# Attention scores from three products of rounded high and low parts, with later query pairs turned in score banks

## The chip, the core and the metric

The program runs on one core of one Trainium2 chip. A core has a matrix engine (TensorE, PE in the profile; PEld is its weight load), a vector engine (VectorE, DVE), an activation engine (ScalarE, ACT), GpSimd (POOL), a queue engine that issues most transfers (SyncE, SP), an on-chip memory of 128 partitions, and eight banks of 128x512 float32 in which matmul results land. The metric is the device time of the whole program in microseconds (us), the median of some runs.

## What is computed

A first block of two layers (retention and gated recurrence, then 16 experts), and a second block of two layers on the same 256 tokens: a pooling layer, then an attention layer, each followed by a multilayer perceptron. The change is in the attention layer:

```
q_l, k_l, v_l = qkv_project(h_lat, w_qkv, g_q, g_k)      # 8 query heads, 2 key heads, 128 wide
q_l = apply_axial_rope(q_l, tables)
k_l = apply_axial_rope(k_l, tables)
q_c, k_c, v_c = qkv_project(h_ctx, w_qkv, g_q, g_k)      # 256 context tokens
k_all = jnp.concatenate([k_c, k_l], axis=1)              # 512 keys
...
s = einsum(q, k) * (HEAD_DIM ** -0.5)
p = softmax(s)
o = einsum(p, v)
```

## The kernel before

Each engine has its instructions written out by hand in one order, and semaphores join them. The expert part runs to about 1380 us and waits mostly for weights. Then come the pooling layer, its perceptron, the attention layer from about 1594 us to 1705 us, and the last perceptron, which runs to the end.

**Attention, ahead of its loop.** PE projects the 256 tokens (two tiles `t` of 128) to keys, values and queries (L1502). DVE norms and rotates the rows (`k_rows`, `q_rows`); the last quarter of the queries is rotated by POOL, after DVE's reciprocal that signals `q_inverse_ready`. PE turns rows to columns by transposes against an identity: `turn_keys` (L1529) fills one bank, which DVE copies to `kT2`, and `turn_queries(pair, bank)` (L1546) fills a bank with two heads, which ACT copies to `qT2` (`query_copies`). The context keys' half of `kT2` was made in the same way during the last expert (`ckT`, L1300).

**The loop.** There are 16 units `u`: 8 heads by 2 tiles of queries. For each, PE forms 128x512 scores in one float32 matmul (`scores(u)`, L1566; a float32 matmul shows as two records). DVE takes the row maximum (`score_max`), ACT the exponential with its sum (`exponentials`), DVE the reciprocal of the sum and the scaling (the row `prob<-prob,softmax_stat`), PE turns the 128x512 result (`turn_probs`, L1575), and ACT copies it to `probT` (`turned_probs`). After each second unit PE multiplies with the values (`values(head)`, L1587). Scores are made two units ahead, in banks 0, 1, 6, 7 in turn; turned probabilities use banks 2 and 3, values banks 4 and 5. Query pair 0 is turned ahead of the loop in bank 2, pair 1 in bank 3, pairs 2 and 3 at units 3 and 7 in bank 5.

```
for u in range(NQ * NT):                      # DVE
    freed(dve, ("s", u))
    step(reciprocal(soft[:, u % 4, 3:4], soft[:, u % 4, 2:3]))
    ts(pr[:, u % 2, :], pr[:, u % 2, :], soft[:, u % 4, 3:4], None, ...
    if u + 2 < NQ * NT:
        score_max(u + 2)
    if u >= 3 and u % 2:
        take_values((u - 3) // 2)
```

After the loop the output product uses rounded parts already: `product` (L628 to L630) adds high times high, high times low and low times high in one bank. A rounded copy has the type `fp32r`.

A bank that `take` hands out again waits until its readers have freed it (`readers` counts them). DVE, ACT and POOL instructions are issued through `InTurn` (L515), so that line stands for most of their rows.

Of the kernel before, what the change touches and what calls it, by code (L numbers as in the profile page):

```python
# [23 lines left out]
ALU = mybir.AluOpType  # L24
# [8 lines left out]
P = 128  # L33
# [19 lines left out]

QUERIES_TURNED = {3: 2, 7: 3}

# [82 lines left out]
def build_program(nc, x, cols, w_in, w_out, w_router, w_gate, w_up, w_down, final_g, ctx_x, w_ada,  # L138
# [144 lines left out]
    rope_c = place("rope2_sb", [P, 2, NT, P])  # L283
    gqk = place("gqk_sb", [P, 2, P])
    x_high = place("x_high", [P, KC, S], F32R, where="xT2")
    x_low = place("x_low", [P, KC, S], F32R, where="x_full")
# [14 lines left out]
    at[0] = here["xs2"]  # L301
    qT2 = place("qT2", [P, NQ, S])
    pr = place("prob", [P, 2, 2 * S])
# [4 lines left out]
    at[0] = here["consts_sb"] + 4 * CONSTS["decay"][0]  # L308
    kT2 = place("kT2", [P, NKV, 2 * S])
    cv = place("ctx_v", [P, NT, NKV * P])  # L310
# [166 lines left out]
    def free(ins, name):  # L477

        ins.then_inc(bank_free[where_is[name][0]], 1)
# [110 lines left out]
    def _(pe):  # L590
# [947 lines left out]
        def turn_queries(pair, bank):  # L1538

            pe.wait_ge(S_("q_rot_ready"), 3 + pair // 2)  # L1540
            name = ("qT", pair)
            ps = take(pe, name, bank)
            for head in (2 * pair, 2 * pair + 1):
                for t in range(NT):
                    at_ = (head % 2) * S + t * P
                    ins = turn(ps[:, at_:at_ + P], qr[:, t, head * P:(head + 1) * P], ident)  # L1546
            fill(ins, name)
# [14 lines left out]
        def scores(u):  # L1562
            head, t = divmod(u, NT)
            name = ("s", u)
            ps = take(pe, name, (0, 1, 6, 7)[u % 4])
            ins = mm(ps[:, :], qT2[:, head, t * P:(t + 1) * P], kT2[:, head // 4, :],  # L1566
                     start=True, stop=True)
            fill(ins, name)
# [37 lines left out]
        for u in range(NQ * NT):  # L1606
# [4 lines left out]
            if u in QUERIES_TURNED:  # L1611
                turn_queries(QUERIES_TURNED[u], 5)
            if u + 2 == NQ * NT:
# [34 lines left out]
    def _(act):  # L1648
# [494 lines left out]
        def query_copies(pair):  # L2143

            name = ("qT", pair)
            ps = full(act, name)
            free(f(qT2[:, 2 * pair:2 * pair + 2, :], ps[:, :].rearrange("p (a t) -> p a t", a=2),
                   ACT.Copy), name)

# [74 lines left out]
    def _(dve):  # L2224
# [113 lines left out]
        for l in range(DEPTH):  # L2338
# [278 lines left out]
            if l == 0:  # L2617
                gains(0, 1, "g_mlp_pre")

            def ctx_normalise():  # L2620
                normalise(NT, lambda t: cx[:, t, :], lambda t: cxn[:, t, :], "ctx_rows_ready",
                          first=2)
# [18 lines left out]
            def ctx_step(e):  # L2641
# [24 lines left out]
                elif (l, e) == (1, 15):  # L2666
                    ps = full(dve, "ckT")
                    free(copy(kT2[:, :, S:2 * S], ps[:, :].rearrange("p (g s) -> p g s", g=NKV)),
                         "ckT")

# [292 lines left out]
        def wo_low(n, q):  # L2963
# [3 lines left out]
            tt(low, whole, high.bitcast(F32), ALU.subtract).then_inc(S_("wo_low_ready"), 1)  # L2967

        k_rows(0)
        even_modulated(1)  # L2970
# [6 lines left out]
        q_rows(1, 0)  # L2977
        ps = full(dve, "kT")
        free(copy(kT2[:, :, 0:S], ps[:, :].rearrange("p (g s) -> p g s", g=NKV)), "kT")
        wo_low(0, 3)  # L2980
        q_sums(1, 1)

# [20 lines left out]
        for u in range(NQ * NT):  # L3003
            freed(dve, ("s", u))
            step(reciprocal(soft[:, u % 4, 3:4], soft[:, u % 4, 2:3]))
            ts(pr[:, u % 2, :], pr[:, u % 2, :], soft[:, u % 4, 3:4], None,
               ALU.mult).then_inc(S_("prob_ready"), 1)
            if u + 2 < NQ * NT:
                score_max(u + 2)
            if u >= 3 and u % 2:  # L3010
                take_values((u - 3) // 2)
# [412 lines left out]
```

## Time and profile before

| what | value |
|---|---|
| median of 3 runs | 1902.17 us (1901.84 to 1902.9) |
| profiled execution, its own time | 1903.21 us |
| span of that execution | 1901.4 us |
| PE busy | 1666.8 us, 88% of the span |
| DVE busy | 797.3 us, 42% |
| ACT busy | 524.6 us, 28% |
| POOL busy | 26.8 us, 1% |
| transfers | 626.74 MB, 330 GB/s on average |

The profile is of one execution. Its own time is the span and 1.8 us that lie around it. A share of busy time is a mean over stages of different kinds: the attention layer, on which the change bears, is about 110 us of the span.

### The profile page before, as it was taken

Reading aid. Unit: us, or ns where it says so; the run is one execution under the profiler, and the core shown is the slowest. Engines: PE = TensorE matmul, PEld = TensorE weight load, DVE = VectorE, ACT = ScalarE, POOL = GpSimd, SP = SyncE. Lnnn points to the kernel's source line nnn. Section 1 sums busy time; section 2 is a strip of 40 time slices with the busy share of each in tenths; the row PEclk is TensorE's granted clock in tenths of the full one; section 3 lists DMA queues with packets and bytes.
Section 4 is the critical chain, followed back from the end, with each engine's and each line's share of the span. In section 5 each row is a group of like instructions: output and inputs, shape, how many; then the busy total and the mean of one; then the engine's idle time right before and its main releaser. Section 6 shows DMA issues by size and latency. Waiting matters only on the chain.

```text
span 1901.4 us, 26299 instructions
## 1 busy us (share of the span) xinstructions
PE 1666.8 (88%) x10930; PEld 1117.0 (59%) x10930; DVE 797.3 (42%) x1211; ACT 524.6 (28%) x800; POOL 26.8 (1%) x30
## 2 busy tenths in 40 slices
PE   8999876689789789999778888866799999999998
PEld 7878433245355248786343543522389996568997
DVE  6696302001111037893201111120077676657776
ACT  6434312000000045352100000021274343564443
POOL 0000000000000000000000000000020000100000
PEclk9999988899999889999989999988999999999999
DMA  9888999999999999779999999999965464325551
GB/s 371 307 292 330 378 423 427 422 425 424 419 427 421 427 405 339 260 280 367 428 423 421 426 421 422 425 428 422 416 230 184 176 225 173 133 86 181 178 193 48
DMA packets 128183, 626.74 MB, mean 330 GB/s; under 512 B 7379, under 2 KB 10067, under 8 KB 102614
## 3 DMA queue, kind: packets, MB, share of 16 engines
q1 hardware_dynamic: 127506, 625.02, 82.1%
q8 instruction: 73, 1.20, 0.3%
q10 hardware_dynamic: 580, 0.33, 0.1%
q14 instruction: 24, 0.20, 0.0%
HBM read 622.18 MB, written 3.15 MB: 329 GB/s over the span
## 4 chain that ended last, share of the span: by engine, by line
PE 54%; DMA 35%; DVE 6%; ACT 3%; issue 1%; SPq 1%; POOL 0%; DVEq 0%; ACTq 0%
DMA ring<-in_w_up 16%; PE bank L628 10%; PE bank L630 10%; PE bank L629 10%; DMA ring<-in_w_mlp_in 8%; DMA ring<-in_w_mlp_out 5%; PE bank L1251 5%; DMA ring<-in_w_down 5%; PE bank L1102 5%; PE bank L1269 4%; PE bank L1502 2%; DVE w_low L515 1%; PE bank L645 1%; PE bank L1145 1%; PE bank L845 1%
## 5 line engine op out<-in xcount | busy, mean ns | idle before, releaser
L1102 PE MATMUL bank<-ring,xeT 128*32 128x512 f32 x1920 | 258.5, 684 | 97.9 <-DMA ring<-in_w_up 97.5
L1102 PEld LDWEIGHTS bank<-ring,xeT 128*32 128x32 f32 x1920 | 67.3, 118 | 276.4 <-issue 276.0
L515 ACT ACTIVATE silu_g<-bank 128x256 f32<-128x256 f32 x32 | 12.3, 383 | 684.6 <-PE bank L1102 684.6
L515 DVE TENSOR_TENSOR hid_e<-silu_g,bank 128x256 f32<-128x256 f32 x32 | 13.5, 421 | 365.6 <-ACT silu_g L515 365.6
L2812 DVE TENSOR_TENSOR w_low<-ring,w_high 128x1024 fp32r<-128x1024 f32 x128 | 152.8, 1234 | 9.6 <-ACT w_high L2055 7.1
L2055 ACT ACTIVATE w_high<-ring 128x1024 fp32r<-128x1024 f32 x128 | 126.6, 1050 | 86.8 <-PE bank L630 85.0
L628 PE MATMUL bank<-x_high,w_high 128*128 128x256 f32 x512 | 144.4, 282 | 2.0 <-DVE x_low L515 1.3
L1251 PE MATMUL bank<-ctx_xT,ring 128*128 128x256 f32 x512 | 123.3, 406 | 25.9 <-DMA ring<-in_w_mlp_in 25.9
L1145 PE MATMUL bank<-ring,hid_T 128*32 128x256 f32 x1920 | 118.1, 389 | 30.1 <-DMA ring<-in_w_down 24.7
L629 PE MATMUL bank<-x_low,w_high 128*128 128x256 f32 x512 | 144.1, 281 | 0.0
L630 PE MATMUL bank<-x_high,w_low 128*128 128x256 f32 x512 | 144.1, 281 | 0.0
L1269 PE MATMUL bank<-ring,ctx_hid 128*128 128x512 f32 x256 | 123.1, 643 | 23.9 <-DMA ring<-in_w_mlp_out 23.9
L1251 PEld LDWEIGHTS bank<-ctx_xT,ring 128*128 128x128 f32 x512 | 104.3, 205 | 46.1 <-DMA ring<-in_w_mlp_in 30.2
L515 DVE TENSOR_TENSOR w_low<-ring,w_high 128x2048 fp32r<-128x2048 f32 (+1 forms) x56 | 111.3, 1988 | 12.4 <-ACT w_high L515 7.1
L628 PE MATMUL bank<-w_high,xs_high 128*128 128x512 f32 x256 | 104.2, 407 | 3.1 <-DVE w_low L515 2.8
L1269 PEld LDWEIGHTS bank<-ring,ctx_hid 128*128 128x128 f32 x256 | 52.1, 207 | 92.9 <-issue 64.3
L1145 PEld LDWEIGHTS bank<-ring,hid_T 128*32 128x32 f32 x1920 | 57.5, 111 | 80.8 <-DMA ring<-in_w_down 36.5
L630 PE MATMUL bank<-w_high,xT_low 128*128 128x512 f32 x256 | 101.1, 395 | 0.0
L628 PE MATMUL bank<-w_high,hid_high 128*128 128x512 f32 x256 | 101.0, 395 | 0.0
L630 PE MATMUL bank<-w_high,hid_low 128*128 128x512 f32 x256 | 101.0, 394 | 0.0
L629 PE MATMUL bank<-w_low,xs_high 128*128 128x512 f32 x256 | 101.0, 394 | 0.0
L629 PE MATMUL bank<-w_low,hid_high 128*128 128x512 f32 x256 | 100.9, 394 | 0.0
(302 smaller groups left out, 2590.9 us busy)
## 6 DMA issues: line engine op xcount, KB each, us to landing
ring<-in_w_up SPq DMA_DIRECT2D x60, 2048.0 KB, 24.4
ring<-in_w_gate SPq DMA_DIRECT2D x60, 2048.0 KB, 21.5
ring<-in_w_down SPq DMA_DIRECT2D x58, 2048.0 KB, 30.2
ring<-in_w_ada SPq DMA_DIRECT2D x24, 2048.0 KB, 11.7
ring<-in_w_mlp_in SPq DMA_DIRECT2D x24, 2048.0 KB, 8.4
ring<-in_w_mlp_out SPq DMA_DIRECT2D x24, 2048.0 KB, 7.9
ring<-in_w_in SPq DMA_DIRECT2D x16, 2048.0 KB, 10.4
ring<-in_w_out SPq DMA_DIRECT2D x4, 2048.0 KB, 7.8
```

The lines of the kernel that those rows point to most:

```text
L515: self.ins, self.mine = op(*args, **kw), "none"
L628: mm(ps, lh, rh, start=first, stop=False, skip_group_check=True)
L629: mm(ps, lh, rl, start=False, stop=False, skip_group_check=True)
L630: return mm(ps, ll, rh, start=False, stop=last, skip_group_check=True)
L645: ins = mm(ps[32 * g:32 * g + 32, :], cT[:, at_:at_ + 32], w[:, 2 * g + k, :], start=(n, k) == (0, 0), stop=(n, k) == (len(batch) - 1, 1), ...
L1102: ins = mm(ps[32 * j:32 * j + 32, :], xeT[:, g % 2, c, i * CAP:(i + 1) * CAP], w[:, :, k, j, :, :], start=c == 0, stop=c == KC - 1, skip_g ...
L1145: ins = mm(banks[q // 2][rows_, at_:at_ + 256], hidT[:, j, 32 * block:32 * block + 32], w[:, c, 256 * q:256 * (q + 1)], start=(n, c) == (0 ...
L1251: ins = mm(ps[:, (j % 2) * S:(j % 2 + 1) * S], w[:, c, j * P:(j + 1) * P], cxT[:, c, :], start=c == 0, stop=c == KC - 1)
L1269: ins = mm(ps[:, :], chid[:, c, t * P:(t + 1) * P], w[:, c, half * 512:(half + 1) * 512], start=c == 0, stop=c == 3)
L1502: ins = mm(ps[:, :], xT2[:, c, t * P:(t + 1) * P], w[:, c, :], start=c == 0, stop=c == KC - 1)
L2055: raw(w_high[:, n % 2, quarter(q)], ring[:, slot, quarter(q)], ACT.Copy).then_inc(S_("w_high_ready"), 1)
L2812: nc.vector.tensor_tensor(w_low[:, slot, quarter(q)], ring[:, slot, quarter(q)], w_high[:, n % 2, quarter(q)].bitcast(F32), ALU.subtract). ...
```

## The change

Scores are formed as three products of `fp32r` parts, as the output product is. `kT2` and `qT2` become the rounded high parts, and `k_low` and `q_low` hold the remainders. DVE makes the remainders by subtraction from the bank in which the turned rows lie (`keys_split`, `queries_low`); ACT still makes the rounded copy of the queries. A bank of turned queries has two readers now, ACT and then DVE. Query pairs 2 and 3 are turned at units 4 and 8, in the score bank that the next scores will use, and no more in bank 5.

```diff
-QUERIES_TURNED = {3: 2, 7: 3}
+QUERIES_TURNED = {4: 2, 8: 3}
+SCORE_BANKS = (0, 1, 6, 7)
...
+    k_low = place("k_low", [P, NKV, 2 * S], F32R)
+    q_low = place("q_low", [P, NQ, S], F32R, where="ctx_y")
...
-    qT2 = place("qT2", [P, NQ, S])
+    qT2 = place("qT2", [P, NQ, S], F32R)
...
-    kT2 = place("kT2", [P, NKV, 2 * S])
+    kT2 = place("kT2", [P, NKV, 2 * S], F32R)
...
-            ps = take(pe, name, bank)
+            ps = take(pe, name, bank, readers=2)
...
-            ps = take(pe, name, (0, 1, 6, 7)[u % 4])
-            ins = mm(ps[:, :], qT2[:, head, t * P:(t + 1) * P], kT2[:, head // 4, :],
-                     start=True, stop=True)
+            ps = take(pe, name, SCORE_BANKS[u % 4])
+            rows_, g = slice(t * P, (t + 1) * P), head // 4
+            ins = product(ps[:, :], (qT2[:, head, rows_], q_low[:, head, rows_]),
+                          (kT2[:, g, :], k_low[:, g, :]), True, True)
...
-                turn_queries(QUERIES_TURNED[u], 5)
+                turn_queries(QUERIES_TURNED[u], SCORE_BANKS[(u + 3) % 4])
...
+            def keys_split(name, cols_):
+
+                keys = full(dve, name)[:, :].rearrange("p (g s) -> p g s", g=NKV)
+                tick(copy(kT2[:, :, cols_], keys))
+                free(tt(k_low[:, :, cols_], keys, kT2[:, :, cols_].bitcast(F32), ALU.subtract),
+                     name)
...
-                    ps = full(dve, "ckT")
-                    free(copy(kT2[:, :, S:2 * S], ps[:, :].rearrange("p (g s) -> p g s", g=NKV)),
-                         "ckT")
+                    keys_split("ckT", slice(S, 2 * S))
...
+        def queries_low(pair):
+
+            name, heads = ("qT", pair), slice(2 * pair, 2 * pair + 2)
+            sem, value = read_by[name]
+            dve.wait_ge(sem, value - 1)
+            ps = full(dve, name)
+            free(tt(q_low[:, heads, :], ps[:, :].rearrange("p (a t) -> p a t", a=2),
+                    qT2[:, heads, :].bitcast(F32), ALU.subtract), name)
...
-        ps = full(dve, "kT")
-        free(copy(kT2[:, :, 0:S], ps[:, :].rearrange("p (g s) -> p g s", g=NKV)), "kT")
+        keys_split("kT", slice(0, S))
         wo_low(0, 3)
+        queries_low(0)
         q_sums(1, 1)
...
+            if u == 0:
+                queries_low(1)
+            elif u in QUERIES_TURNED:
+                queries_low(QUERIES_TURNED[u])
             if u + 2 < NQ * NT:
                 score_max(u + 2)
```

Three places show how instructions stand before and after. (The lines of the changed kernel are three further down, so L518 answers to L515, L631 to L633 to the three products, L1549 to L1546, L1579 to L1575 and L1591 to L1587.) The first is DVE just ahead of the loop, from the copy of the turned keys to the first row maximum and the reciprocal for POOL; before:

```order
L515 COPY kT_154<-bank 128x2x256
L515 TENSOR_TENSOR w_low<-ring,w_high 128x1024
L515 TENSOR_REDUCE q_stat<-q_square 128x4
L515 TENSOR_REDUCE softmax_stat<-bank 128x1
L515 TENSOR_SCALAR softmax_stat<-softmax_stat 128x1
L515 RECIPROCAL q_stat<-q_stat 128x4
```

Of the change, in the same place:

```order
L518 CAST kT_156<-bank 128x2x256
L518 TENSOR_TENSOR k_low<-bank,kT_156 128x2x256
L518 TENSOR_TENSOR w_low<-ring,w_high 128x1024
L518 TENSOR_TENSOR q_low<-bank,qT_150 128x512
L518 TENSOR_REDUCE q_stat<-q_square 128x4
L518 TENSOR_REDUCE softmax_stat<-bank 128x1
L518 TENSOR_SCALAR softmax_stat<-softmax_stat 128x1
L518 RECIPROCAL q_stat<-q_stat 128x4
```

Two subtractions now stand ahead of the reduction to `q_stat`, for which ACT's square root, its table load and the first exponential wait in turn, and the first scores of PE wait for the second of them.

The second place is PE in the loop, from the turned probabilities of unit 2 (before) to those of unit 4:

```order
L1575 MATMUL bank<-consts_sb,prob 128x128 x4
L1566 MATMUL bank<-kT_154,qT_148 128x512
L1546 MATMUL bank<-consts_sb,q_rot 128x128 x4
L1575 MATMUL bank<-consts_sb,prob 128x128 x4
L1566 MATMUL bank<-kT_154,qT_148 128x512
L1587 MATMUL bank<-probT,kv 128x256 x2
L1587 MATMUL bank<-probT,ctx_v 128x256 x2
L1575 MATMUL bank<-consts_sb,prob 128x128 x4
```

Of the change:

```order
L1579 MATMUL bank<-consts_sb,prob 128x128 x4
L631 MATMUL bank<-kT_156,qT_150 128x512
L632 MATMUL bank<-k_low,qT_150 128x512
L633 MATMUL bank<-kT_156,q_low 128x512
L1579 MATMUL bank<-consts_sb,prob 128x128 x4
L631 MATMUL bank<-kT_156,qT_150 128x512
L632 MATMUL bank<-k_low,qT_150 128x512
L633 MATMUL bank<-kT_156,q_low 128x512
L1549 MATMUL bank<-consts_sb,q_rot 128x128 x4
L1591 MATMUL bank<-probT,kv 128x256 x2
L1591 MATMUL bank<-probT,ctx_v 128x256 x2
L1579 MATMUL bank<-consts_sb,prob 128x128 x4
```

The turn of query pair 2 (`q_rot`) moved from ahead of the turned probabilities of unit 3 to behind the scores of unit 6, just ahead of the value products, whose bank it no more uses.

The third place is DVE in units 4 and 5, from the reciprocal of unit 4 on; before:

```order
L515 RECIPROCAL softmax_stat<-softmax_stat 128x1
L515 TENSOR_SCALAR prob<-prob,softmax_stat 128x512
L515 TENSOR_REDUCE softmax_stat<-bank 128x1
L515 TENSOR_SCALAR softmax_stat<-softmax_stat 128x1
L515 RECIPROCAL softmax_stat<-softmax_stat 128x1
L515 TENSOR_SCALAR prob<-prob,softmax_stat 128x512
```

Of the change:

```order
L518 RECIPROCAL softmax_stat<-softmax_stat 128x1
L518 TENSOR_SCALAR prob<-prob,softmax_stat 128x512
L518 TENSOR_TENSOR q_low<-bank,qT_150 128x512
L518 TENSOR_REDUCE softmax_stat<-bank 128x1
L518 TENSOR_SCALAR softmax_stat<-softmax_stat 128x1
L518 RECIPROCAL softmax_stat<-softmax_stat 128x1
L518 TENSOR_SCALAR prob<-prob,softmax_stat 128x512
```

A subtraction of 128x512 from a bank stands between the two scalings of a pair of units here; in units 0 and 8 it is the same.

## Rows read from the trace of the kernel before

**Rows 1.** The page's chain that ended last: shares of the span by engine.

```profile
PE 54%; DMA 35%; DVE 6%; ACT 3%; issue 1%; SPq 1%; POOL 0%; DVEq 0%; ACTq 0%
```

**Rows 2.** Stretches: start:end, length, busy us by engine, PE clock, DMA share.

```profile
1639.90:1642.30 2.40, 0.03 (x1) 0.04 (x1) 1.95 (x4) 2.17 (x6) 2.24 (x3) 1.00 1.05 406
1666.00:1670.70 4.70, 4.62 (x21) 2.87 (x21) 3.39 (x10) 3.13 (x7) 0.00 (x0) 1.00 0.01 3
```

**Rows 3.** Timeline of one pair in the loop: start, duration, engine, line, operation.

```profile
1666.82 0.16 DVE L515 RECIPROCAL softmax_stat<-softmax_stat 128x1 f32<-128x1 f32 x1 [0.73 <-ACT prob L515]
...
1668.23 1.02 PE L1566 MATMUL bank<-kT,qT 128*128 128x512 f32 x2
...
1668.79 0.49 DVE L515 TENSOR_SCALAR prob<-prob,softmax_stat 128x512 f32<-128x512 f32 x1
1669.33 0.66 PE L1575 MATMUL bank<-consts_sb,prob 128*128 128x128 f32 x4
...
1670.03 0.60 ACT L515 ACTIVATE probT<-bank 128x512 f32<-128x512 f32 x1 [0.24 <-PE bank L1575]
...
1670.74 0.69 ACT L515 ACTIVATE prob<-bank,softmax_stat 128x512 f32<-128x512 f32 x1
...
1671.55 0.16 DVE L515 RECIPROCAL softmax_stat<-softmax_stat 128x1 f32<-128x1 f32 x1 [0.73 <-ACT prob L515]
```

**Rows 4.** The chain of waits in the loop, one piece: start, length, what.

```profile
1663.71 0.86 PE bank L1566 x2
```

**Rows 5.** Timeline of PE in the output product behind the loop.

```profile
1676.29 0.50 PE L628 MATMUL bank<-w_high,o_high 128*128 128x512 f32 x1 [1.58 <-ACT prob L515]
...
1676.63 0.39 PE L629 MATMUL bank<-w_low,o_high 128*128 128x512 f32 x1
...
1676.86 0.39 PE L630 MATMUL bank<-w_high,o_low 128*128 128x512 f32 x1
```

**Rows 6.** Timeline of DVE and ACT ahead of the loop.

```profile
1634.53 0.69 DVE L515 COPY kT<-bank 128x512 f32<-128x512 f32 x1
...
1635.32 1.23 DVE L515 TENSOR_TENSOR w_low<-ring,w_high 128x1024 fp32r<-128x1024 f32 x1
...
1637.52 0.69 DVE L515 TENSOR_REDUCE q_stat<-q_square 128x4 f32<-128x512 f32 x1 [0.97 <-ACT q_square L515]
...
1638.31 0.69 DVE L515 TENSOR_REDUCE softmax_stat<-bank 128x1 f32<-128x512 f32 x1
...
1638.63 1.28 ACT L515 ACT_TABLE_LOAD   x1
```

**Rows 7.** Timeline of DVE: a 128x512 bank with an operand in on-chip memory.

```profile
1394.18 0.68 DVE L515 TENSOR_TENSOR y<-bank,gate_rows 128x512 f32<-128x512 f32 x1
```

**Rows 8.** Timeline of POOL and DVE at the first two scalings.

```profile
1639.55 1.04 POOL L515 TENSOR_TENSOR q_raw<-q_raw,q_stat 128x512 f32<-128x512 f32 x1 [45.09 <-DVE q_stat L515]
...
1640.67 1.26 POOL L515 TENSOR_TENSOR q_tmp<-q_raw,rope_gained 128x512 f32<-128x512 f32 x1
...
1640.94 1.27 DVE L515 TENSOR_SCALAR prob<-prob,softmax_stat 128x512 f32<-128x512 f32 x1
...
1643.49 0.49 DVE L515 TENSOR_SCALAR prob<-prob,softmax_stat 128x512 f32<-128x512 f32 x1
...
1644.37 1.26 POOL L515 TENSOR_TENSOR q_rot<-q_tmp 128x512 f32<-128x512 f32 x1
```

**Rows 9.** Timeline of PE: value products that begin a pair of units.

```profile
1645.43 1.10 PE L1587 MATMUL bank<-probT,kv 128*128 128x256 f32 x4
...
1651.03 1.10 PE L1587 MATMUL bank<-probT,kv 128*128 128x256 f32 x4 [0.61 <-ACT qT L515]
...
1655.71 1.10 PE L1587 MATMUL bank<-probT,kv 128*128 128x256 f32 x4
```

**Rows 10.** Timeline of PE in the last expert, behind the context keys.

```profile
1354.49 5.51 PE L1102 MATMUL bank<-ring,xeT 128*32 128x512 f32 x32 [3.57 <-DMA ring<-in_w_up]
```

**Rows 11.** A stretch of the last expert, columns as in the second group.

```profile
1354.50:1359.90 5.40, 5.40 (x32) 1.33 (x32) 0.00 (x0) 0.00 (x0) 0.00 (x0) 0.67 1.00 425
```

More of the change, by code:

```diff
@@ L2146, in query_copies @@
             ps = full(act, name)
-            free(f(qT2[:, 2 * pair:2 * pair + 2, :], ps[:, :].rearrange("p (a t) -> p a t", a=2),
-                   ACT.Copy), name)
+            sem, value = read_by[name]
+            f(qT2[:, 2 * pair:2 * pair + 2, :], ps[:, :].rearrange("p (a t) -> p a t", a=2),
+              ACT.Copy).then_inc(sem, 1, value - 1)
         for t in range(NT):
@@ L2967, in wo_low @@
             tt(low, whole, high.bitcast(F32), ALU.subtract).then_inc(S_("wo_low_ready"), 1)
+        def queries_low(pair):
+            name, heads = ("qT", pair), slice(2 * pair, 2 * pair + 2)
+            sem, value = read_by[name]
+            dve.wait_ge(sem, value - 1)
+            ps = full(dve, name)
+            free(tt(q_low[:, heads, :], ps[:, :].rearrange("p (a t) -> p a t", a=2),
+                    qT2[:, heads, :].bitcast(F32), ALU.subtract), name)
         k_rows(0)
```

## The prediction

> **What bounds the kernel now.** First the chain that ended last: over the whole program it is on PE for 54% and on transfers for 35% [rows 1]. The change touches one stage, the attention loop, so the next view is the stretch of one pair of units there: in 4.70 us PE is busy 4.62, DVE 3.39, ACT 3.13 [rows 2]. By these shares PE looks like the bound, and a cheaper score matmul like a gain. The timeline of that pair says otherwise [rows 3]. Follow what starts when the thing before it ends: DVE's reciprocal of the even unit at 1666.82, then DVE without a pause (scaling, maximum, reciprocal, scaling) to 1668.79 + 0.49 = 1669.28; PE's turn of the odd unit at 1669.33; ACT's copy at 1670.03; ACT's exponential at 1670.74; DVE's next reciprocal at 1671.55. That closes a loop of 1671.55 - 1666.82 = 4.73 us per pair, through DVE, one turn on PE and two steps of ACT. The scores are not in it: those ahead of the odd turn start at 1668.23 and take 0.86 [rows 3, 4], so they are done at 1669.09, 0.19 before the probabilities that the turn waits for. PE is full, and still it waits a little for DVE in each pair.
>
> **The change, part by part.**
>
> *Scores.* Before: 0.86 a unit [rows 4]. After: three `fp32r` products. The output product has the same three with the same shapes; they start at 1676.63 and 1676.86, 0.23 apart, and the whole takes 1676.86 + 0.39 - 1676.29 = 0.96 from a standing start [rows 5]. In a stream that is 3 x 0.23 = 0.69, or 0.17 less for each of 16 units, 2.7 in all. On the path it is worth nothing by the loop above: scores that were 0.19 early become 0.36 early. Its bounds are nothing and, if all 14 in the loop were on the path, 14 x 0.17 = 2.4. I take 0.
>
> *Context keys.* One more subtraction, in the last expert. A 128x512 operation on a bank and an operand takes 0.68 there [rows 7], and the next value products of PE wait for it. Behind them PE waits 3.57 for `w_up` anyway [rows 10], which hides it: 0. Without that cover it would be 0.8.
>
> *Ahead of the loop.* Two subtractions, `k_low` and `q_low` of pair 0. Each takes 0.68 [rows 7], and dependent DVE operations stand about 0.1 apart: the copy of the keys starts at 1634.53, the next at 1635.32, a step of 0.79 [rows 6]. So 1.58. DVE idles 0.97 before the reduction to `q_stat` because ACT is late [rows 6]; less the ordinary 0.1 that covers 0.87. The rest is 1.58 - 0.87 = +0.71. What is late next: ACT's square root, then its table load (now to 1638.63 + 1.28 + 0.71 = 1640.62), then the first exponential. PE's first scores wait for `q_low` too, until 1635.32 + 0.79 + 1.23 + 0.1 + 0.69 = 1638.13; with 0.96 they end at 1639.1, and their maximum, then at 1639.15 and done by 1640.1, is in time for ACT at 1640.62. So +0.71 and no more.
>
> *POOL against the first scaling.* The reciprocal that starts POOL stands behind that first maximum, which moves from 1638.31 [rows 6] to 1639.15: POOL starts 0.84 later. The first scaling took 1.27 against 0.49 for the second, and it ended at 1642.21, 0.28 after the POOL operation that runs from 1640.67 to 1641.93 [rows 8]: it looks held by that operation. After: POOL's operation is at 1641.51 to 1642.77 and the scaling asks at 1640.94 + 0.71 = 1641.65, behind its start again, so it ends 0.28 after 1642.77, at 1643.05: +0.84 where 0.71 was counted, +0.13 more. Were the scaling first by a hair, it would take 0.49 and end at 1642.14, 0.78 less than counted. So between -0.78 and (held from the start of the operation) +0.27; I take +0.13, since the margin is 0.14. The Trainium skill has a rule for this: "SBUF — State Buffer", section "SBUF: two separate sides", says that VectorE in its two-port mode and GpSimd take a shared pair of ports by an exclusive lock, for a whole instruction, whoever starts first. The first scaling agrees with it; the second, 0.49 long within POOL's run, does not show a wait.
>
> *`q_low` of pair 1, in unit 0.* It stands between two scalings, on DVE's part of the loop, and ACT's copy is done by then: +0.79, with nothing to hide it.
>
> *Pairs 2 and 3.* Before, a pair of units with a turn lasts 1651.03 - 1645.43 = 5.60 and the next 1655.71 - 1651.03 = 4.68 [rows 9], so a turn cost 0.87 to 0.92 over the ordinary 4.73. The value products waited 0.61 for ACT's copy of the queries, which lay in their bank [rows 9], and that copy stood before the exponential on which DVE waits. After, the bank is another, the copy falls between the two exponentials of a pair (ACT has 4.70 - 3.13 = 1.57 to spare [rows 2]), and PE's turn takes the time that the products save. But DVE does one more subtraction on its part of the loop, 0.79. So 0.79 - 0.9 = -0.1 each, -0.2 for two. If ACT's copy were not hidden, 0.7 each would come back (0.60 for a copy from a bank [rows 3] and a gap), +1.4.
>
> *Sum.* 0.71 + 0.13 + 0.79 - 0.2 + 0 + 0 = +1.43 us, a shift of all that follows, since the output product and the perceptron begin only when the loop ends. The profiled execution took 1903.21, so 1904.6 for its like; it lies 1.04 above the median of the three runs. On the median 1902.17 the sum gives **1903.6**. What a measurement of this kernel can tell from no change is 0.2%, 3.8 us: the forecast is no measurable change.
>
> **The rivals.**
>
> *The scores are on the path.* For it: the chain of waits has pieces of 0.86 on the score line [rows 4], and PE is busy 4.62 of 4.70. Against it: the 0.19 to spare. Six such pieces would give 6 x 0.17 = 1.0 back: 1902.6; all 14 would give 1901.2, which the 0.19 makes too unlikely for the range. Chance 0.12.
>
> *The first scaling slips in before POOL.* The margin is 0.14. Then 0.91 less, 1902.7. Chance 0.16.
>
> *The second scaling is held too.* It asks at 1643.49 + 0.71 + 0.13 + 0.79 = 1645.12, and POOL's last operation moves from 1644.37 to 1645.21 and lasts 1.26 [rows 8]. It should be first by 0.09. If not, it ends 0.28 after 1646.47 and not at 1645.61, +1.14: 1904.7. By the rule of the Trainium skill named above this is just the collision to fear, since the one that starts first keeps the ports. Chance 0.13.
>
> *ACT's copies in units 4 and 8 are not hidden*: +1.4, 1905.0. Chance 0.05.
>
> *PE's clock falls (the other side).* The loop now runs at the full 2.4 GHz, after an idle stretch of 2.40 us with the clock at 1.00 [rows 2]. After the change PE idles for up to 1.6 before the first scores (the two added steps of DVE) and again until the first turn (from 1640.9, some 1.8 after the first scores end, to 1643.1): 3.8 us in two pieces where it was 2.4 in one. In the last expert, after 3.57 idle [rows 10], the next 5.40 us had a mean of 0.67 [rows 11], which is 5.40 x 0.33 x 2 = 3.6 us at 1.2 GHz. PE has hardly any slack in a pair, so that would lose about 3.6 / 2 = 1.8, to 1905.4. It decides for slower when more than 3.8 - 1.4 = 2.4 is lost, that is from 4.8 us at the low clock, two such falls: 1907.2. Against it: each idle piece is shorter than the one that left the clock alone. The Trainium skill, "TensorE: Matmul & The Clock Gate", section "Part 1: The HAM clock gate", says that the half clock is the state at rest and activity lifts it, which speaks against any new idle time on PE; the 2.40 us did not bring it about here. Chance 0.07, of which 0.03 beyond the bound.
>
> *The change doesn't do what it says*: three products at float32's price, 3 x 0.43 = 1.29 a unit. A pair on PE would take 4.62 + 0.86 = 5.5, PE would bound the loop, and 7 pairs would lose 0.75 each, with the 1.4 that is +6.7: 1908.9. The output product's 0.23 speaks against it. Chance 0.02. What I have not seen, on either side: 0.02 for a gain beyond the bound.
>
> **How the numbers follow.** The forecast itself keeps 0.43. The cases from 1902.6 to 1905.0 together have 0.89. The three runs before spread over 1.06 us, so I widen by about half of that on the low side and reach 1905.2 on the high side, short of the falling clock: 1902.0 to 1905.2. Faster by over 0.2%: 0.02. Slower: 0.03 and 0.02, say 0.05. Same: 0.93.
>
> **What would show it.** In the changed profile: score products 0.23 apart, PE less busy in a pair, and the period of an ordinary pair still 4.73. The reduction to `q_stat` about 0.7 later than its place behind the key copy now (2.99 after its start). The first scaling again near 1.27. Pairs with a turn near 5.5. The prediction is wrong if ordinary pairs get shorter (the scores were on the path), if the granted clock of the loop is under 1.00, or if the time that follows the loop changes its length.

## The result, and the profile after

The changed kernel took 1905.82 us in the median of 15 runs (1903.7 to 1908.48); the kernel before, run beside it, took 1902.86 in the median of 15 (1900.93 to 1907.04). The ratio is 1.0017 with an interval of 1.001 to 1.0024, which is 1.9 to 4.6 us slower. The ratio itself lies inside the 0.2% that the prediction called no measurable change, though its interval leaves out 1 and reaches 0.24%. The median lies above the range of the prediction, which ended at 1905.2. The predicted loss was 1.43 us, and the difference of the medians is 2.96. The base moved too: the forecast was counted from a median of 3 runs, 1902.17, which is 0.69 below the 1902.86 of the 15.

The spans of the two profiled executions (1901.4 and 1903.1) are a poor measure of this change: the stage happened to begin about 3 us earlier in the execution after (over all the executions below it begins anywhere from 1631.41 to 1637.24). So everything below is counted from DVE's copy of the keys, where the stage begins (1634.53 before [rows 6], 1631.58 after). The distance from there to the first output product behind the loop is called **the stage** from here on, and the yardstick in the recorded expectations: 1676.29 - 1634.53 = 41.76 before [rows 5], 1677.93 - 1631.58 = 46.35 after. From the key copy to the end it is 266.87 and 271.52, so the loss of 4.6 us between these two executions arises in the stage; behind it both take the same (225.11 and 225.17).

The page's chain of the kernel after, shares by engine (it answers to [rows 1]):

```profile
PE 55%; DMA 33%; DVE 7%; ACT 3%; issue 1%; SPq 0%; DVEq 0%; POOL 0%; ACTq 0%
```

The timeline of the kernel after ahead of the loop and through its first two units, all engines together; the helper's line has moved from L515 to L518:

```profile
1631.58 0.69 DVE L518 CAST kT<-bank 128x512 fp32r<-128x512 f32 x1
1632.30 0.69 DVE L518 TENSOR_TENSOR k_low<-bank,kT 128x512 fp32r<-128x512 f32 x1
...
1634.46 0.69 DVE L518 TENSOR_TENSOR q_low<-bank,qT 128x512 fp32r<-128x512 f32 x1
1635.20 0.50 PE L631 MATMUL bank<-kT,qT 128*128 128x512 f32 x1 [1.30 <-DVE q_low L518]
1635.25 0.69 DVE L518 TENSOR_REDUCE q_stat<-q_square 128x4 f32<-128x512 f32 x1
...
1635.54 0.40 PE L632 MATMUL bank<-k_low,qT 128*128 128x512 f32 x1
...
1635.77 0.39 PE L633 MATMUL bank<-kT,q_low 128*128 128x512 f32 x1
...
1638.47 0.16 DVE L518 RECIPROCAL softmax_stat<-softmax_stat 128x1 f32<-128x1 f32 x1
...
1638.56 3.47 POOL L518 TENSOR_TENSOR q_tmp<-q_raw,rope_gained 128x512 f32<-128x512 f32 x5
1638.67 1.44 DVE L518 TENSOR_SCALAR prob<-prob,softmax_stat 128x512 f32<-128x512 f32 x1
...
1640.24 0.69 DVE L518 TENSOR_TENSOR q_low<-bank,qT 128x512 fp32r<-128x512 f32 x1
...
1642.11 1.26 POOL L518 TENSOR_TENSOR q_rot<-q_tmp 128x512 f32<-128x512 f32 x1
1642.22 1.44 DVE L518 TENSOR_SCALAR prob<-prob,softmax_stat 128x512 f32<-128x512 f32 x1
...
1643.71 1.12 PE L1579 MATMUL bank<-consts_sb,prob 128*128 128x128 f32 x4 [2.20 <-DVE prob L518]
```

Read beside [rows 6, 8]: the reduction to `q_stat` has no idle time ahead of it any more and starts 1635.25 - 1631.58 = 3.67 after the key copy, where it was 2.99. The first scaling takes 1.44 where it took 1.27. The second takes 1.44 where it took 0.49: POOL's `q_rot` began 0.11 before it, and the scaling ended at 1643.66, 0.29 after `q_rot` did (1643.37). The score products stand 0.23 apart from the second on, as in the output product [rows 5].

Then PE slows down. Stretches of 2 us of the kernel after from there on (columns as in [rows 2]; the column behind the five engines is PE's granted clock):

```profile
1639.58:1641.58 2.00, 1.35 (x7) 0.88 (x7) 1.76 (x3) 1.04 (x3) 1.69 (x5) 1.00 0.71 267
1641.58:1643.58 2.00, 0.00 (x0) 0.00 (x0) 1.83 (x4) 0.00 (x0) 1.72 (x2) 0.72 0.00 1
1643.58:1645.58 2.00, 1.87 (x7) 1.63 (x8) 0.92 (x3) 0.60 (x2) 0.00 (x0) 0.50 0.00 0
1645.58:1647.58 2.00, 2.00 (x6) 1.58 (x5) 1.05 (x3) 1.55 (x4) 0.00 (x0) 0.50 0.04 8
1647.58:1649.58 2.00, 2.00 (x8) 1.52 (x7) 1.09 (x4) 0.00 (x0) 0.00 (x0) 0.58 0.00 0
1649.58:1651.58 2.00, 2.00 (x14) 1.65 (x13) 0.85 (x2) 1.46 (x3) 0.00 (x0) 1.00 0.00 0
```

The second row is PE's idle stretch while the second scaling is held. The clock falls in it to 0.50, the lower of its two levels (1.2 GHz), and is back at 1.00 only in the last row. The turn of the second unit's probabilities takes 1.12 where an undisturbed one takes 0.66.

The later loop of the kernel after: the reciprocals that begin a pair with a turn and the next pair, the subtraction of that pair's queries, the value products that begin two ordinary pairs, the first output product that ends the stage, and the stretch of one ordinary pair:

```profile
1652.63 0.16 DVE L518 RECIPROCAL softmax_stat<-softmax_stat 128x1 f32<-128x1 f32 x1 [0.56 <-ACT prob L518]
...
1653.45 0.69 DVE L518 TENSOR_TENSOR q_low<-bank,qT 128x512 fp32r<-128x512 f32 x1
...
1658.18 0.16 DVE L518 RECIPROCAL softmax_stat<-softmax_stat 128x1 f32<-128x1 f32 x1 [0.73 <-ACT prob L518]
...
1667.63 1.10 PE L1591 MATMUL bank<-probT,kv 128*128 128x256 f32 x4
...
1672.36 1.10 PE L1591 MATMUL bank<-probT,kv 128*128 128x256 f32 x4
...
1677.93 0.50 PE L631 MATMUL bank<-w_high,o_high 128*128 128x512 f32 x1 [1.58 <-ACT prob L518]
```

```profile
1667.00:1671.70 4.70, 4.43 (x24) 3.25 (x22) 3.40 (x9) 3.11 (x8) 0.00 (x0) 1.00 0.01 2
```

An ordinary pair lasts 1672.36 - 1667.63 = 4.73, as before [rows 3], though PE is now busy 4.43 of 4.70 where it was 4.62 [rows 2]. A pair with a turn lasts 1658.18 - 1652.63 = 5.55. Between the same reciprocals it was 1651.81 - 1646.25 = 5.56 in the kernel before (the 5.60 of [rows 9] is measured between value products):

```profile
1646.25 0.16 DVE L515 RECIPROCAL softmax_stat<-softmax_stat 128x1 f32<-128x1 f32 x1 [1.29 <-ACT prob L515]
...
1651.81 0.16 DVE L515 RECIPROCAL softmax_stat<-softmax_stat 128x1 f32<-128x1 f32 x1 [1.56 <-ACT prob L515]
```

In the last expert the context keys' subtraction is over long before the next weights land, and PE waits for the same weights as before [rows 10]:

```profile
1343.21 0.69 DVE L518 TENSOR_TENSOR k_low<-bank,kT 128x512 fp32r<-128x512 f32 x1
...
1349.82 6.58 PE L1105 MATMUL bank<-ring,xeT 128*32 128x512 f32 x32 [1.86 <-DMA ring<-in_w_up]
```

From PE's turn of the context keys to this matmul it is 8.01 in the kernel before and 8.03 after, so the subtraction costs nothing there. The 6.58 of the matmuls, 5.51 before, is not the change's: the kernel with only the turns moved (e2 below), whose context keys are as before, has 6.58 too.

### The profile page after: what moved, and what is told of

Same layout as the page of the kernel before. It is cut to its first block, busy times and chain, and to the rows that moved or that the text cites. A ratio compares the mean times of both kernels' runs of the same rounds, so it can differ in the third digit from the quotient of the medians.

```text
span 1903.1 us, 26341 instructions
## 1 busy us (share of the span) xinstructions
PE 1674.2 (88%) x10946; PEld 1124.3 (59%) x10946; DVE 802.8 (42%) x1217; ACT 524.9 (28%) x800; POOL 27.1 (1%) x30
## 4 chain that ended last, share of the span: by engine, by line
PE 55%; DMA 33%; DVE 7%; ACT 3%; issue 1%; SPq 0%; DVEq 0%; POOL 0%; ACTq 0%
DMA ring<-in_w_up 12%; PE bank L631 10%; PE bank L633 10%; PE bank L632 10%; DMA ring<-in_w_mlp_in 9%; PE bank L1254 7%; DMA ring<-in_w_mlp_out 6%; PE bank L1272 5%; DMA ring<-in_w_down 5%; PE bank L1105 4%; PE bank L1505 2%; DVE w_low L518 1%; PE bank L648 1%; PE bank L1148 1%; PE bank L848 1%
## 5 line engine op out<-in xcount | busy, mean ns | idle before, releaser
L1105 PE MATMUL bank<-ring,xeT 128*32 128x512 f32 x1920 | 263.8, 697 | 89.1 <-DMA ring<-in_w_up 88.9
L518 ACT ACTIVATE silu_g<-bank 128x256 f32<-128x256 f32 x32 | 12.3, 384 | 679.6 <-PE bank L1105 679.6
L518 DVE TENSOR_TENSOR hid_e<-silu_g,bank 128x256 f32<-128x256 f32 x32 | 13.5, 421 | 362.1 <-ACT silu_g L518 362.1
L631 PE MATMUL bank<-x_high,w_high 128*128 128x256 f32 x512 | 144.7, 283 | 1.5 <-DVE x_low L518 1.1
L633 PE MATMUL bank<-x_high,w_low 128*128 128x256 f32 x512 | 144.4, 282 | 0.0
L518 DVE TENSOR_TENSOR w_low<-ring,w_high 128x2048 fp32r<-128x2048 f32 (+1 forms) x56 | 111.3, 1988 | 14.1 <-ACT w_high L518 8.8
L631 PE MATMUL bank<-w_high,xs_high 128*128 128x512 f32 x256 | 104.3, 407 | 3.0 <-DVE w_low L518 2.7
L518 ACT ACTIVATE w_high<-ring 128x2048 fp32r<-128x2048 f32 (+1 forms) x56 | 93.6, 1671 | 28.6 <-DMA ring<-in_w_in 23.1
L633 PE MATMUL bank<-w_high,xT_low 128*128 128x512 f32 x256 | 101.0, 395 | 0.0
L631 PE MATMUL bank<-w_high,hid_high 128*128 128x512 f32 x256 | 101.0, 395 | 0.0
L633 PE MATMUL bank<-w_high,hid_low 128*128 128x512 f32 x256 | 101.0, 395 | 0.0
```

Of the source, the lines that this page charges most:

```text
L518: self.ins, self.mine = op(*args, **kw), "none"
L631: mm(ps, lh, rh, start=first, stop=False, skip_group_check=True)
L633: return mm(ps, ll, rh, start=False, stop=last, skip_group_check=True)
L1105: ins = mm(ps[32 * j:32 * j + 32, :], xeT[:, g % 2, c, i * CAP:(i + 1) * CAP], w[:, :, k, j, :, :], start=c == 0, stop=c == KC - 1, skip_g ...
```

## The experiments

Theory going in: the added work of DVE costs 0.68 ahead of the loop, 0.17 by the shift of POOL against the first scaling, 0.83 for `q_low` in unit 0 and 0.95 because the second scaling is held by POOL; the turned pairs come out even. Together 2.63, so a stage of 44.4. The remaining 1.96 of the profiled execution is PE's clock. Rivals: the three products cost time themselves; the clock is the whole loss. The runs have the labels e1 to e11.

**The changed kernel again** (e1, no edit).

> The changed kernel as it is, a second look. Yardstick of all these runs: from the start of DVE's copy of the turned keys to the first matmul of the output product, 41.76 us before and 46.35 after (+4.59). Theory (idle and port): 0.68 for the two subtractions ahead of the loop, 0.17 for POOL starting later, 0.83 for the subtraction of pair 1, 0.95 for the second scaling held by POOL, 0 for the moved turns, and 1.96 for PE at half clock behind its two idle stretches. If the fall of the clock is set by the idle stretches it is seen again, 46.3 within 0.5; if it is chance, a run without it shows 44.4. Rival (work alone): all 4.59 is DVE's added work, the same 46.35 with a full clock.

The stage took 46.30, the two scalings 1.44 and 1.45, and the clock fell in the same place to 0.50. There is one time, 1910.48, and from one execution nothing follows for the median. The fall was seen twice in two executions, so it is not a single accident.

**Only the turns moved** (e2), scores in float32 as before.

```diff
--- before
-QUERIES_TURNED = {3: 2, 7: 3}
+QUERIES_TURNED = {4: 2, 8: 3}
+SCORE_BANKS = (0, 1, 6, 7)
...
-                turn_queries(QUERIES_TURNED[u], 5)
+                turn_queries(QUERIES_TURNED[u], SCORE_BANKS[(u + 3) % 4])
```

> The kernel before with query pairs 2 and 3 turned at units 4 and 8 in score banks, and float32 scores as before. With no subtraction on DVE, ACT's copy of the queries leaves the chain of the loop: theory says the two pairs of units with a turn fall from 5.56 us to 4.73, the yardstick from 41.76 to about 40.1, the clock stays at 1.00, and the time falls by 1.6 us, 0.1%. Rival: the turn itself costs PE its 0.44 us in each, 41.0.

1901.76, ratio 0.9991 (0.9982 to 1.0001). The stage took 40.98. The timeline of DVE, the reciprocals around the first turned pair, and the two stretches of 2 us that begin just behind the start of its first turn of probabilities:

```profile
1645.77 0.16 DVE L516 RECIPROCAL softmax_stat<-softmax_stat 128x1 f32<-128x1 f32 x1 [1.50 <-ACT prob L516]
...
1650.65 0.16 DVE L516 RECIPROCAL softmax_stat<-softmax_stat 128x1 f32<-128x1 f32 x1 [0.52 <-ACT prob L516]
...
1655.41 0.16 DVE L516 RECIPROCAL softmax_stat<-softmax_stat 128x1 f32<-128x1 f32 x1 [0.52 <-ACT prob L516]
```

```profile
1641.39:1643.39 2.00, 2.00 (x8) 0.84 (x7) 1.29 (x4) 0.60 (x1) 1.69 (x5) 0.60 0.70 263
1643.39:1645.39 2.00, 2.00 (x6) 1.24 (x5) 0.84 (x2) 1.02 (x2) 1.11 (x1) 0.54 0.00 0
```

A turned pair takes 1655.41 - 1650.65 = 4.76 here, within 0.03 of an ordinary one. So the new place of the turns does save 5.56 - 4.76 = 0.80 in each of two pairs, and in the changed kernel the subtraction of the queries' low part (5.55) takes it all back. The clock fell here too, with PE idle 2.40 ahead of the first turn, as long as in the kernel before, whose profiled execution kept the full clock [rows 2]. That fall lengthened the first two pairs by 0.80 (6.16 and 4.88, where they would be 5.51 and 4.73), so the 40.98 meets the rival's 41.0 by luck: the turned pairs of 4.76 and 40.98 - 0.80 = 40.2 lie near the 4.73 and 40.1 of the theory.

**Small matmuls in PE's two idle stretches** (e3) of the changed kernel (their results are not read).

```diff
--- after
+        keep_clock_narrow("unread_scores", 4, 12)
         freed(pe, ("qT", 0))
...
+            if u == 0:
+                keep_clock_narrow("unread_probs", 4, 18)
             turn_probs(u)
```

> The changed kernel with 12 small matmuls on PE ahead of the first scores and 18 ahead of the first turned probabilities, into a bank that nobody reads. Theory (idle): the clock of the loop stays at 1.00, the yardstick falls by 1.96 from 46.35 to 44.4. Rival (the fp32r products themselves or chance bring the clock down): the clock falls as before, 46.3 or more.

1905.8, ratio 1.0015 (1.0006 to 1.0025). The clock stayed at 1.00 through the loop, but the matmuls were too many and pushed the first reciprocal from 6.89 to 7.98 after the key copy. The stage took 45.52; less that 1.09 it is 44.43, the 44.4 of the theory. Whole times could not show it, and in the profiled execution a clock that fell in the perceptron cost another 1.1 (226.22 from the first output product to the end, 225.11 before).

**POOL held back** (e4) until both scalings are done.

```diff
--- after
         pool.wait_ge(S_("q_inverse_ready"), 1)
+        pool.wait_ge(S_("prob_ready"), 2)
```

> The changed kernel with POOL's rotation of the last queries started only after the second scaling. Theory (port): the first and second scalings take 0.49 us each and not 1.44, the yardstick falls by 1.9 to 44.4, and by up to 1.96 more (to 42.5) if the shorter idle stretch of PE leaves the clock at 1.00. Some later scaling may be held by up to 1 us in their place. Rival (the scalings are slow for another reason, a first use of the tile): they stay at 1.44 and the yardstick at 46.3.

1904.74, ratio 1.0004 (0.9995 to 1.0014). The timeline of DVE and POOL:

```profile
1640.43 0.49 DVE L518 TENSOR_SCALAR prob<-prob,softmax_stat 128x512 f32<-128x512 f32 x1
...
1643.02 0.49 DVE L518 TENSOR_SCALAR prob<-prob,softmax_stat 128x512 f32<-128x512 f32 x1
...
1643.65 1.04 POOL L518 TENSOR_TENSOR q_raw<-q_raw,q_stat 128x512 f32<-128x512 f32 x1 [50.38 <-DVE prob L518]
```

Both scalings take 0.49, the clock in the loop is 1.00 and the stage is 42.50, so POOL costs the changed kernel 44.4 - 42.5 = 1.9: that the two scalings are held by POOL is shown. The turned pairs take 5.55 as in the changed kernel. In this execution PE's clock fell just behind the loop instead (a mean of 0.57 over the 4 us from the first output product on), which gave back about 1.6: from there to the end it took 226.77, and 225.11 before.

**One product per score** (e5). The scores are one float32 matmul of the rounded parts; the low parts are computed but not used, so the scores are those of rounded queries and keys.

```diff
--- after
-            ins = product(ps[:, :], (qT2[:, head, rows_], q_low[:, head, rows_]),
-                          (kT2[:, g, :], k_low[:, g, :]), True, True)
+            ins = mm(ps[:, :], qT2[:, head, rows_].bitcast(F32), kT2[:, g, :].bitcast(F32),
+                     start=True, stop=True)
```

> The changed kernel with scores as one float32 matmul of the rounded high parts (the two products with low parts are left out of the computation, the subtractions that make them stay). Scores cost PE 0.86 us a unit again and not 0.69. Theory (scores off the path): ordinary pairs of units stay at 4.73 us and the yardstick at 46.3 within 0.3, if the clock falls as it did, or 44.4 if it stays. Rival (scores on the path): each ordinary pair is 0.3 longer, the yardstick 2.4 longer at the same clock.

1905.37, ratio 1.0014 (1.0005 to 1.0023). The stage took 44.53, ordinary pairs 4.73 and turned ones 5.55, all with the clock at 1.00. Scores at float32's price and scores as three products give the same pairs: they are off the path, and the loss at the full clock is in DVE's work and its wait for POOL. (The 0.14 over 44.39, the stage of the changed kernel at the full clock found below, lies ahead of the loop: the first reciprocal is at 7.04 behind the key copy and not at 6.90.)

**The queries' subtractions in odd units** (e6; units 1, 5 and 9, with the turns in banks 5 and 4), so that they stand behind the second scaling of a pair.

```diff
--- after
-        turn_queries(1, 3)
+        turn_queries(1, 5)
...
-                turn_queries(QUERIES_TURNED[u], SCORE_BANKS[(u + 3) % 4])
+                turn_queries(QUERIES_TURNED[u], 4)
...
-            if u == 0:
+            if u == 1:
                 queries_low(1)
-            elif u in QUERIES_TURNED:
-                queries_low(QUERIES_TURNED[u])
+            elif u - 1 in QUERIES_TURNED:
+                queries_low(QUERIES_TURNED[u - 1])
```

> The changed kernel with the subtractions of pairs 1, 2 and 3 one unit later, behind the scaling of units 1, 5 and 9, where DVE idles 0.73 us for ACT, and with the turned queries in banks 5 and 4. Theory: each is then hidden, 3 x 0.83 = 2.5 less, and the second scaling comes before POOL's last operation and takes 0.49 (0.95 less): the yardstick goes from 46.35 to 42.9 with a fall of the clock like the one seen, to 40.9 without. Rival (work alone): DVE's work is the same, so the yardstick stays within 0.5 of 46.35.

1903.82, ratio 1.0001 (0.9991 to 1.0012). The timeline of DVE and POOL:

```profile
1645.79 0.49 DVE L518 TENSOR_SCALAR prob<-prob,softmax_stat 128x512 f32<-128x512 f32 x1
1646.41 0.69 DVE L518 TENSOR_TENSOR q_low<-bank,qT 128x512 fp32r<-128x512 f32 x1
...
1646.67 1.27 POOL L518 TENSOR_TENSOR q_rot<-q_tmp 128x512 f32<-128x512 f32 x1
```

The second scaling is first by 0.88 now and takes 0.49, and the subtraction from a bank, which begins 0.26 before POOL's `q_rot` and overlaps it, takes its usual 0.69. The turned pairs took 4.93 and 5.12 instead of 5.55, not quite hidden. The stage was 42.39, though the clock fell here too (0.63 and 0.51 over 4 us). It fell again behind the loop, and from the key copy to the end this execution took 269.12, where the kernel before has 266.87.

**The same, with the last subtraction of weights (`wo_low(0, 3)`) moved behind the loop** (e7), which takes 1.23 of DVE out of the way of `q_low`.

```diff
--- the kernel with the subtractions in odd units
-        wo_low(0, 3)
         queries_low(0)
...
+        wo_low(0, 3)
         take_values(NQ - 1)
```

> As e6, and DVE's fourth low quarter of the output weights, 1.33 us, goes from ahead of the loop to its end. Theory: the two subtractions ahead of the loop are covered, the reduction to q_stat is back at 2.99 us behind the copy of the keys (3.67 in the change), the yardstick is another 0.68 less: 42.2 with a fall of the clock, 40.2 without, against 41.76 before; the time is that of the kernel before or up to 1.6 less. Rival: PE's wait for the low part of the first queries still delays the first scores, and the yardstick gains nothing on e6.

1902.55, ratio 0.9997 (0.9988 to 1.0006). The reduction to `q_stat` is back at 2.99, the first pair at 5.52, and the stage is 40.88, 0.88 shorter than before. It misses the 40.2 of the expectation by the turned pairs (4.93 and 5.28). In each of them PE's turn of the queries waited 0.28 for `o_low`, which frees its bank, and later scores waited 0.24 and 0.34 for `q_low`; what each wait costs no run shows. So the three products can stand in this stage at no loss, with their DVE work in the gaps. The whole gained nothing: behind the stage this execution took 0.86 longer than the kernel before, with the clock down to 0.50 in the perceptron (as e5 did, which lost 0.85 there without the move), and from the key copy to the end it took 266.85. Ahead of the first turn PE was idle longer here than in any other run, and the clock stayed at 1.00 through the whole stage:

```profile
1641.49 0.66 PE L1579 MATMUL bank<-consts_sb,prob 128*128 128x128 f32 x4 [2.66 <-DVE prob L518]
```

**The same with POOL held back** (e8), by the same added wait as above.

> As e7, and POOL's rotation starts only after the second scaling. Theory: the first scaling takes 0.49 too, PE's idle stretch ahead of the first turn shortens by 0.8 and the clock stays: yardstick 39.4 against 41.76 before, time 2.3 us less than before, 0.12%. Rival: another scaling or the turn of the last queries waits for POOL, 40.2 or more.

1903.52, ratio 0.9999 (0.999 to 1.0008). The stage was 40.18, the expected 0.8 less than the last (but 0.8 above the forecast, by the turned pairs once more). The profiled execution gained no time by it, for the clock fell in the next stretch. PE's first output product, and stretches of 2 us from there:

```profile
1674.95 0.50 PE L631 MATMUL bank<-w_high,o_high 128*128 128x512 f32 x1 [1.58 <-ACT prob L518]
```

```profile
1675.00:1677.00 2.00, 2.00 (x6) 1.61 (x7) 1.23 (x4) 0.78 (x2) 0.00 (x0) 0.67 0.04 8
1677.00:1679.00 2.00, 2.00 (x6) 1.54 (x5) 0.00 (x0) 0.00 (x0) 0.00 (x0) 0.50 0.00 0
```

From the key copy to the end it took 266.93, as the kernel before.

**Small matmuls in the idle stretches of both kernels** (e9 is the kernel before, e10 the changed one), fewer than above. Both have 6 ahead of the first output product. Ahead of the first turned probabilities there are 9 in e9 and 8 in e10, and e10 has 5 more ahead of the first scores. The edit of e9:

```diff
--- before
+                keep_clock_narrow("unread_wo", 4, 6)
                 take(pe, ("wo", 0, 0), 6, readers=2)
...
+            if u == 0:
+                keep_clock_narrow("unread_probs", 4, 9)
             turn_probs(u)
```

That of e10 is the same with 8 for 9, and one line more ahead of the first scores, `keep_clock_narrow("unread_scores", 4, 5)`.

> The kernel before with small matmuls into an unread bank in PE's idle stretches: 9 ahead of the first turned probabilities, 6 ahead of the first output product. So far the clock fell inside the loop in some executions and not in others, of the change and of kernels with the idle stretch of the kernel before. Theory (falls by chance, more of them after the change): the clock of the loop stays at 1.00, the yardstick is 41.8 as in the clean execution of before, and the time is that of before or up to 1 us less. Rival (before has no falls to speak of): the same time as before to 0.3 us.

> The changed kernel with fillers of the right length: 5 ahead of the first scores, 8 ahead of the first turned probabilities, 6 ahead of the first output product (a small one took 0.215 us before, and the too long ones held the scores up by 1.09). Theory: clock at 1.00, yardstick 44.4, that is 46.35 less the 1.96 of the fall; 2.6 us slower than e9, whose clock is held too. Rival (the fall is not caused by idle time): the clock falls in the loop again, 46.3.

The times are 1902.53 (ratio 1.0, 0.9991 to 1.0009) and 1906.37 (1.0019, 1.001 to 1.0028). Both kept the full clock throughout the stage, with their first reciprocals where they were without the added matmuls (6.22 and 6.90). The ends of the stage, first in e9 and then in e10:

```profile
1633.78 0.69 DVE L515 COPY kT<-bank 128x512 f32<-128x512 f32 x1
...
1675.56 0.50 PE L628 MATMUL bank<-w_high,o_high 128*128 128x512 f32 x1 [0.24 <-ACT prob L515]
```

```profile
1633.99 0.69 DVE L518 CAST kT<-bank 128x512 fp32r<-128x512 f32 x1
...
1678.38 0.50 PE L631 MATMUL bank<-w_high,o_high 128*128 128x512 f32 x1 [0.24 <-ACT prob L518]
```

The stage took 41.78 and 44.39, so with the clock equal the change costs 2.61, where the four steps add up to 2.63. The clock is not the whole loss, then. The whole times did not shrink with it: 1906.37 is no less than the changed kernel's 1905.82, and it is 3.84 above e9, where the expectation had 2.6. The time of e9 does not tell its theory from its rival. Stretches of the changed kernel with added matmuls, around its second idle stretch and in the perceptron behind the loop:

```profile
1643.99:1645.99 2.00, 0.00 (x0) 0.00 (x0) 1.83 (x4) 0.00 (x0) 1.71 (x2) 1.00 0.02 8
1645.99:1647.99 2.00, 1.83 (x9) 1.36 (x10) 0.93 (x3) 1.06 (x2) 0.00 (x0) 1.00 0.00 0
```

```profile
1716.00:1718.00 2.00, 2.00 (x14) 2.00 (x13) 2.00 (x2) 1.93 (x4) 0.93 (x2) 0.63 1.02 410
1718.00:1720.00 2.00, 2.00 (x12) 2.00 (x11) 1.90 (x4) 2.00 (x3) 1.88 (x2) 0.51 0.54 219
```

The idle stretch before the second unit's turn was 2.18 and left the clock alone here. It fell later, in the perceptron, whose code the change leaves as it was, and cost 1.1 (226.22 from the first output product to the end, where it is 225.11 before).

**Turns moved, POOL held back, small matmuls (6 and 6)** (e11), scores in float32: the parts that had paid, without the change's three products.

> The kernel before with float32 scores, the later pairs turned at units 4 and 8 in score banks, POOL's rotation started after the second scaling, and fillers (6 and 6). Theory: the turns cost nothing (2 x 0.83 less), the first scaling takes 0.49 (0.78 less): yardstick 39.4 against 41.76, the time 2.4 us below that of before, 0.12%. Rival: the turn of the last queries waits for POOL, or fillers delay the turns of probabilities: 40.2 or more.

1900.83, ratio 0.9991 (0.9982 to 1.0), 2.1 us less than the kernel before. Both scalings took 0.49, the clock was 1.00, and the stage was 39.76. It misses the 39.4 by its first turned pair, which took 5.12 where e2 has 4.76: PE's turn of the queries began at 1646.98, right behind POOL's `q_rot`, which ended at 1646.93, so the rival came true in part. It is the fastest of the kernels here and lies at the edge of what the runs can tell from no change.

## Why the prediction was wrong, step by step

**Right:** the scores are off the path (the pair of 4.73 unchanged, and the float32 scores gave the same). The context keys cost 0, by the cover that the prediction named (the matmul of PE that takes their bank next waited 0.46 for `k_low`, inside the wait for `w_up`). The subtractions ahead of the loop: 0.71 predicted, 0.68 measured. POOL against the first scaling: +0.13 predicted, 0.17 measured. `q_low` of pair 1: 0.79 predicted, 0.83 measured (the next maximum went from 7.78 to 9.46 after the key copy, 1.68 in all, less the 0.85 that was there already).

**The step that failed:** the second scaling, of which the prediction said "It should be first by 0.09", with a chance of 0.13 for the contrary. The sum shifted POOL's run as it stood, 0.84 later and as long as before. But that run had been lengthened by the scaling itself. The last two of POOL's five `q_tmp` operations in the kernel before, each in a stretch with the busy time of `q_tmp` alone:

```profile
1643.10:1643.64 0.54, 0.00 (x0) 0.46 (x1) 1.00 0.99 368
1643.64:1644.34 0.70, 0.00 (x0) 0.62 (x1) 1.00 0.30 111
```

and the same two in the kernel after:

```profile
1641.00:1641.54 0.54, 0.00 (x0) 0.46 (x1) 1.00 0.30 114
1641.54:1642.07 0.53, 0.00 (x0) 0.45 (x1) 1.00 0.01 4
```

(The column before the clock is POOL.) Before, the second scaling ran from 1643.49 to 1643.98 [rows 8] and POOL's last `q_tmp`, which began inside it, took 0.62 instead of 0.46. After, the scaling came 0.85 + 0.83 later, past that operation, so POOL's run was 0.16 shorter (3.47, where the timeline of before has 3.63) and `q_rot` 0.16 earlier than the sum had it. That turns 0.09 for the scaling into 0.07 against it; the scaling itself came 0.05 later than the sum, by the three small misses above, and measured it was 0.11 behind. The scaling took 0.95 more, not the 1.14 of that rival. The run's length follows the scalings in each kernel: 3.63 with the subtraction in an odd unit, where the scaling falls into the run again, and 3.79 with POOL held back, where two scalings do. The rule of the Trainium skill that the prediction named, "SBUF — State Buffer", section "SBUF: two separate sides", says that whichever starts first keeps the shared ports for its whole instruction. The traces agree on the order, in both directions: the scaling 0.11 behind POOL took 1.44, and POOL behind the scaling 0.16 more. They do not show a wait in every overlap: the scaling at 1643.49 began about 0.11 before POOL's fourth `q_tmp` ended and still took 0.49. The prediction had used the rule in one direction only. That POOL is what holds both scalings, the runs with POOL held back show: 0.49 each.

**The term that was mis-sized:** the turned pairs, -0.2 predicted and 0.00 measured (5.55 and 5.56 a pair). The saving was 0.80 a pair and not 0.9, which was read between value products (5.60) where the loop of the reciprocals has 5.56, and the subtraction takes the saving back (0.79). With the small misses of the three terms above this makes 2.63 for the 1.43 of the prediction.

**The base:** as a shift the range of the prediction went up to 1905.2 - 1902.17 = 3.03, and the medians of 15 differ by 2.96. The time came out above the range because the median of 3 runs lay 0.69 low; that does not mend the sum, which had 1.43.

**The clock:** put at 0.07 with a cost of 1.8. In the profiled execution it fell and cost 46.35 - 44.39 = 1.96, close to the price that the prediction gave it. The stretch in which it fell, 2.20, is one that the prediction did not have: PE waited there for the held second scaling, where it waited 0.26 before. The argument "each idle piece is shorter than the one that left the clock alone" failed: the 2.40 of the kernel before is no safe length, since the same 2.40 brought the clock down in the kernel with only the turns moved, and 2.17 did so with the subtractions in odd units. Nor is it an unsafe one: 2.66 in e7 left the clock alone. The length of one idle stretch does not decide it in these runs.

**Open:** how much of the measured 1.9 to 4.6 us is the clock. The steps of DVE and POOL alone give 2.63, within the interval, and holding the clock in the stage did not lower the median. Each kernel that does the change's added DVE work showed a fall somewhere between the key copy and 210 us behind the loop, in nine of nine profiled executions, in the loop, just behind it or in the perceptron; of the four without that work one did, and two of the other three had added matmuls. How often it falls in executions that were not profiled no run shows.

## What to carry to other kernels

Where two engines share something, what was measured of the one holds the wait for the other: take it out before shifting it, and price a lead of a tenth of a microsecond as both cases. Price an operation on the engine that closes the loop at its full length, whatever it does for the engine that is merely busiest: PE was 98% busy in a pair, and a fifth less of its score work (0.69 for 0.86) was worth nothing. When a change moves one stage by a few microseconds, measure that stage from an event at its start, since the whole program scatters by more (1900.93 to 1907.04 for the kernel before).

## What the runs showed of the hardware

A DVE scaling in on-chip memory that asks just behind the start of a long POOL operation (1.26) takes 1.43 to 1.47 instead of 0.49 and ends 0.28 to 0.29 after it in the kernels before and after; a POOL operation that begins within a scaling takes 0.62 instead of 0.46; a DVE subtraction from a bank within POOL's run stays at 0.69. PE's clock went to its lower level after idle stretches of 1.58, 2.17, 2.20 and 2.40 us and stayed up after others of 1.58, 2.18, 2.40 and 2.66, in the same places of nearly the same programs; one fall cost 0.8 to 2.0 us. Three `fp32r` products stand 0.23 apart, 0.69 together, in the place of one float32 matmul of 0.86.
